# Weight chunks of 1 MB that arrive in one transfer on one semaphore, in a one-core Trainium2 decoder layer

## The reference

```python
m = silu(c) @ w_ada + b_ada                          # 6 parts of 2048: shift, scale, gate, twice
h = rms_norm(x, g_pre) * (1.0 + scale) + shift
q, k, v, u = split(h @ w_in)                         # 4 x 1024 columns
attn = differential_attention(rotary(q), rotary(k), v, cache_k, cache_v, page_table)   # 8 heads
pooled = windowed_means(u, state_pool) @ w_pool
x = x + gate * rms_norm(concat(rms_norm(attn), pooled) @ w_out, g_post)
h = rms_norm(x, g_pre_ffn) * (1.0 + scale2) + shift2
x = x + gate2 * rms_norm(square(relu(h @ w_ff1)) @ w_ff2, g_post_ffn)   # 2048 -> 8192 -> 2048
```

## Time and profile before

| | |
|---|---|
| median of 3 runs | 1516.92 us (1516.67 to 1517.27) |
| the profiled execution, its own time | 1515.74 us |
| its span in the trace | 1514.1 us |
| PE busy | 1454.0 us, 96% of the span |
| DVE / ACT / POOL busy | 54% / 34% / 7% |
| DMA | 316.22 MB, mean 209 GB/s |
| transfers of the stream | 544 of 512 KB, median 4.9 us from issue to landing |

### The profile page before, as it was taken

One profiled execution on the slowest core, in us unless ns is written; L12 is line 12 of the kernel. 1 busy time (PEld: TensorE's weight loads), 2 busy tenths in 40 slices (PEclk: granted clock), 3 DMA queues, 4 the chain that ended last, 5 costly groups with the idle time before them and its releaser, 6 DMA issues.

```text
span 1514.1 us, 27154 instructions
## 1 busy us (share of the span) xinstructions
PE 1454.0 (96%) x10302; PEld 1322.7 (87%) x10302; DVE 810.3 (54%) x1289; ACT 518.3 (34%) x743; POOL 106.2 (7%) x175
## 2 busy tenths in 40 slices
PE   5999999999899998999999999999999999999994
PEld 1677777778688886999998999999999999999993
DVE  2555558855755568665343544333454434555556
ACT  2222234443455543333323333322333322333331
POOL 1000000067310000000000000000000000000003
PEclk9999999999999999999999999999999999999997
DMA  9999989889587667344445544445544444444421
GB/s 367 331 322 328 318 299 323 278 305 358 209 300 265 242 240 273 121 157 149 156 139 199 191 145 160 144 160 190 188 152 150 155 140 148 157 139 150 156 83 69
DMA packets 87725, 316.22 MB, mean 209 GB/s; under 512 B 12160, under 2 KB 12288, under 8 KB 87024
## 3 DMA queue, kind: packets, MB, share of 16 engines
q1 hardware_dynamic: 79056, 287.87, 54.8%
q0 software_dynamic: 5216, 22.51, 3.9%
q10 hardware_dynamic: 3392, 5.01, 0.9%
HBM read 309.56 MB, written 5.80 MB: 208 GB/s over the span
## 4 chain that ended last, share of the span: by engine, by line
PE 85%; DVE 6%; DMA 5%; issue 1%; ACT 1%; SPq 0%; POOL 0%; POOLq 0%; DVEq 0%; ACTq 0%
PE bank L1471 69%; PE bank L1529 7%; PE bank L1449 4%; DMA raw<-in_stream 4%; DMA k_pages<-in_kc 1%; DVE w_lo L760 1%; PE bank L1675 1%; PE bank L1458 1%; PE bank L1704 1%; ACT w_hi L387 0%; DVE back L325 0%; DVE x L326 0%; DVE pair L1153 0%; PE bank L1626 0%; DVE mixed L1141 0%
## 5 line engine op out<-in xcount | busy, mean ns | idle before, releaser
L387 ACT ACTIVATE w_hi<-raw 128x1024 fp32r<-128x1024 f32 x352 | 361.9, 1055 | 360.7 <-PE bank L1471 233.2
L760 DVE TENSOR_TENSOR w_lo<-raw,w_hi 128x1024 fp32r<-128x1024 f32 x352 | 419.5, 1225 | 119.6 <-ACT w_hi L387 118.4
L1471 PE MATMUL bank<-m_hi,w_hi 128*128 128x320 f32 x1280 | 397.3, 310 | 1.2 <-DVE w_lo L760 0.6
L1471 PE MATMUL bank<-m_hi,w_lo 128*128 128x320 f32 x1280 | 395.5, 309 | 0.0
L1471 PE MATMUL bank<-m_lo,w_hi 128*128 128x320 f32 x1280 | 395.5, 309 | 0.0
L1471 PE MATMUL bank<-h_hi,w_hi 128*128 128x320 f32 x1216 | 380.2, 313 | 3.1 <-ACT relu L661 3.1
L1471 PE MATMUL bank<-h_hi,w_lo 128*128 128x320 f32 x1216 | 376.4, 310 | 0.0
L1471 PE MATMUL bank<-h_lo,w_hi 128*128 128x320 f32 x1216 | 376.3, 309 | 0.0
L1471 PEld LDWEIGHTS bank<-m_hi,w_hi 128*128 128x128 f32 x1280 | 240.3, 188 | 15.2 <-issue 13.7
L1471 PEld LDWEIGHTS bank<-h_hi,w_hi 128*128 128x128 f32 x1216 | 228.8, 188 | 27.4 <-issue 27.4
L1471 PEld LDWEIGHTS bank<-m_lo,w_hi 128*128 128x128 f32 x1280 | 240.3, 188 | 0.0
(11 more groups left out here) (230 smaller groups left out, 1024.2 us busy)
## 6 DMA issues: line engine op xcount, KB each, us to landing
raw<-in_stream SPq DMA_DIRECT2D x544, 512.0 KB, 4.9
k_pages<-in_kc POOLq DMA_DIRECT2D x16, 512.0 KB, 10.1
v_pages<-in_vc POOLq DMA_DIRECT2D x16, 512.0 KB, 7.6
x<-in_x_cm ACTq DMA_DIRECT2D x1, 2560.0 KB, 12.1
x<-in_x_cm POOLq DMA_DIRECT2D x1, 2560.0 KB, 11.7
v_out<-v_cm POOLq DMA_DIRECT2D x1, 1280.0 KB, 9.5
k_out<-back POOLq DMA_DIRECT2D x1, 1280.0 KB, 10.1
y_out<-x SPq DMA_DIRECT2D x2, 640.0 KB, 3.0
```

The costliest lines, as they stand in the source:

```text
L387: act.activation(w_hi[2 * (j % 2) + h][:, :], raw[slot][:, h * 1024:(h + 1) * 1024], ACT.Copy).then_inc(hi_ready, 1)
L760: dve.tensor_tensor(w_lo[q][:, :], raw[slot][:, h * 1024:(h + 1) * 1024], w_hi[q][:, :], ALU.subtract).then_inc(slot_used[slot], 1)
L1471: last = pe.matmul(bank[j % 2][:, 0:T], w[q][:, k * P:(k + 1) * P], v[:, 8 * h + k, :], start=(h == 0 and k == 0 and n == 0), stop=(h == 1 ...
```

## The change

SP issues one transfer of 1 MB for each chunk instead of two of 512 KB, and a slot has one semaphore for loading instead of two. Both halves of ACT's rounding and all four products of an ada chunk wait for that one semaphore, that is for the whole chunk. All counts, the slots, the order of instructions on PE, ACT, DVE and POOL, and the wait of SP before it issues stay as they are. On SP a turn of the loop over four slots has 4 transfers where it had 8, each with rows of 8 KB for a partition where it had 4 KB.

```diff
-    raw_loaded = [[S(f"raw_loaded{s}_{h}") for h in range(2)] for s in range(4)]
+    raw_loaded = [S(f"raw_loaded{s}") for s in range(4)]
...
                 sp.wait_ge(slot_used[s], 2 * i + 2)
-                for h in range(2):
-                    half = slice(h * 1024, (h + 1) * 1024)
-                    sp.dma_start(raw[s][:, half], stream[ds(4 * i + s, 1), :, half].rearrange("a p n -> p (a n)")).then_inc(
-                        raw_loaded[s][h], 16)
+                sp.dma_start(raw[s][:, :], stream[ds(4 * i + s, 1), :, :].rearrange("a p n -> p (a n)")).then_inc(
+                    raw_loaded[s], 16)
...
         def hi_half(c4, use, off, j, h):
             slot, u = use_of(use, off)
-            act.wait_ge(raw_loaded[slot][h], 16 * (u + 1))
+            act.wait_ge(raw_loaded[slot], 16 * (u + 1))
...
             for kk in range(4):
-                if kk % 2 == 0:
-                    pe.wait_ge(raw_loaded[slot][kk // 2], 16 * (u + 1))
+                if kk == 0:
+                    pe.wait_ge(raw_loaded[slot], 16 * (u + 1))
```

## The result

The changed kernel takes **1520.53 us** (median of 22 runs, 1516.33 to 1524.85), the kernel before, run beside it on the same chip, 1516.32 (22 runs, 1511.21 to 1520.61). One run of the changed kernel took 2044 us at a granted clock of 0.65 and is left out of the comparison. The profiled execution took 1522.03 us, its span is 1520.4 us; that is 6.3 us more than the profiled execution of before, and somewhat more than the 4.2 us between the medians.

The account below looks back on a forecast made before the run. PE was taken to set the time, from 43 to 212 us only just ahead of the transfers. Terms of 0.3, 4.0, 2.0, 1.1 and 1.0 gave 8.4 us on 1515.74, a median of 1525.3, range 1517.5 to 1531.5.

Parts of the forecast that it names:

- the pages: K pages at 368.25 us: waiting longer beside the stream's 8 KB rows, 1.0 us, bounds 0 and 2.5.
- the first half's lateness: Whole stream: a chunk's first half is usable only when all has landed; slower, 1521 to 1531 us, chance 0.6.
- start: PE's first product at 43.55 us, behind its chunk's first half: 0.3 us later, bounds 0 and 1.2.
- quarters: 43 to 212 us: PE's columns wait where their slack is less than d; 4.0 us, bounds 0.5 and 7.
- q columns: At 208.91 and 231.84 us, where ACT waited for a half: 2.0 us together, bounds 0.5 and 2.5.
- When all of it lands: Stream: a whole chunk lands 5.1 us after issue, 0.15 us before the second half now; bounds 0 and 0.5.
- d: Quarters: the delay of what stands behind DVE's pair, which ends at 113.20 instead of 112.26 us: 0.94 us.
- the row size gives little: DMA queues from 6 to 12 us: 4 KB and 20 KB rows both cost 0.039 us for a KB.
- rival B: Quarters: loss hidden as PE's slips empty the DMA queue; +1 to +3 us, about 1518.5, chance 0.19.
- rival C: Stream: one transfer saves a fixed part, some 0.9 us a chunk; faster, about 1512.5 us, chance 0.09.
- The first chunk of the output projection: Issued at 418.90 us, with PE starting at 434.70 right after ACT and DVE: 1.1 us, bounds 0.7 and 1.3.
- rival D: Pages, second `x` load, ACT's outputs wait longer beside 8 KB rows, quarters reach upper bound: 1531 to 1535 us, chance 0.12.

Follow-up runs that it names:

- the thinned pages: Changed kernel, and kernel before, each with pages bringing 64 of 1024 columns from the third sequence on: 1512.50 us (ratio 0.9988) and 1513.33 us (0.9993).
- the two others with 8 KB rows: The changed kernel with SP's wait ahead of each issue repeated six times, and 24 times: 1521.81 us (ratio 1.0039) and 1529.31 us (1.0094).

## Why the prediction came out as it did

The time forecast was 1525.3 us with a range of 1517.5 to 1531.5; 1520.53 lies in it, and slower was given 0.73. By its own reasons it was mostly wrong, and that the time lies in the range is luck: the terms that made up 6.3 of its 8.4 us were not there (PE is 2.4 us ahead at 306 us), and the smallest but one, 1.0 for the pages, was several times its size (8.3 us from 306 to 435 us).

**The mechanism of the first half's lateness was right, and even its size, for a chunk that lands when the prediction thought.** The kernel with the old transfers and the whole wait has such a chunk: it lands 5.16 us after its first issue, forecast 5.1. PE is 7.3 us behind with it at 306 us, where the sum had 6.3 (start, quarters and q columns), though it was shared out otherwise: 2.4 at the start instead of 0.3, 2.5 in the quarters instead of 4.0, 2.4 after them instead of 2.0. What the sum did not have is another 6.3 us after 435 us.

**The step that failed is "When all of it lands".** It gave the single transfer a gain of 0.15 us, with 0.5 as the bound. Alone it gains 0.4, and the chunk of the earlier trace rows shows this at one place. The changed kernel issues it at 103.1 us. SP's two issues from 103 to 104 us, the first of them this chunk's (4.7), then ACT and DVE:

```profile
DMA to landing us min/median/max: 4.7/5.5/6.3
```

```profile
107.88 2.01 ACT L385 ACTIVATE w_hi<-raw 128x1024 fp32r<-128x1024 f32 x2 [7.73 <-DMA raw<-in_stream]
```

```profile
108.98 2.36 DVE L758 TENSOR_TENSOR w_lo<-raw,w_hi 128x1024 fp32r<-128x1024 f32 x2 [5.22 <-ACT w_hi L385]
```

The chunk is there 4.7 us after its issue, and DVE's pair ends at 111.34, 8.23 us after the issue; before it ended at 112.26, 7.66 after it. So d was 0.57 us here, not 0.94, and the air of 0.9 took it. But most places are not like this one. The lone chunk of the earlier trace rows was the wrong one to measure: in the quarters the median chunk takes 7.15 us before and 5.65 after, 1.5 less, and less than the first half alone took before, 5.87 us (both from the transfers' records). There d is negative, by the distances of the lone chunk some -0.3 us (an estimate: 5.65 + 3.56 to the end of DVE's pair, before 7.15 + 2.36). Where chunks stand in a queue, two transfers of 4 KB rows hold it longer; the share of the DMA engines fell from 0.92 to 0.83. The step "the row size gives little" rested on the earlier trace rows, six microseconds with two queues at work. The rows of q1 from 43.5 to 212 us, where it has the engines nearly alone, are before, with one transfer of 4 KB rows, and after:

```profile
q1 hardware_dynamic: 14800, 53.87, 91.3%
```

```profile
q1 hardware_dynamic: 13892, 53.56, 85.6%
```

```profile
q1 hardware_dynamic: 7374, 53.62, 82.2%
```

For the same bytes that is a tenth less time on the engines, 0.169 us for 4 KB instead of 0.187 (share times 16 engines times 168.5 us, by the bytes). The kernel between has 0.176: the single transfer gives 0.011 of it and the longer rows 0.007, so the row size does give little, some 4%. What the step left out is what two transfers in place of one cost in a queue.

**The quarters, 4.0 us, and the q columns, 2.0,** therefore came out as nothing or a small gain: PE is 1.7 us further ahead at 214 us than at 45, and level from there to 306. That is rival B's outcome for the quarters, though for another reason than B's (a queue that empties as PE slips), and part of rival C's saving: C wanted 0.9 us a chunk to make the kernel faster, and 0.4 alone and 1.5 in the queue came. The Trainium skill's rule quoted with it ("DMA: Bandwidth & Descriptors", "Anatomy of one DMA"), some 2 us fixed for a transfer and 436 GB/s, would by an estimate give 4.4 us for a chunk alone; 4.8 was measured, between it and the forecast's 5.1. The statement "I would be wrong if PE's idle time in the quarters doesn't grow" came true.

**The start, 0.3:** -0.6 at 45 us, not told from 0. **The first chunk of the output projection, 1.1:** from its issue to PE's start there are 16.6 us (424.05 to 440.64), before 15.8, so 0.8; right.

**The pages, 1.0 with 2.5 as the bound, are the step that carried the loss.** The mechanism stood there, turn by turn and packet by packet, and the queues confirm it. The size failed in three ways. It counted one K page load on the path, and V pages and POOL's later ones came too. It counted two chunks beside the pages. But while both queues have work the pages lose a third of their rate, 0.14 MB in a us instead of 0.21, and four transfers of K pages issued together (two sequences', two pages each) are 2.1 MB: by an estimate from these rates 15 us instead of 10 if the stream is there all along. And it had no term for the clock, which was down at 363 us, after PE had waited. From 347 to 363 us the changed kernel loses 5.2 us, of which 2.7 are there at 360 us, where the K pages have just come, and 2.5 are lost in the 3 us of work behind them, at half clock; from 397 to 405 us it is 3.9. This is rival D's first half (pages and other queues waiting longer) with rival B's quarters. D was priced 1531 to 1535 because it was added to the forecast's terms; by itself it is 1521.

That the 8 KB rows beside the pages cause the loss is shown, by the kernel in which only those rows are shorter and by the thinned pages. How the 8 us divide between waiting and clock is read from one execution, and the two others with 8 KB rows lose 7.1 and 3.4 at somewhat different places. That two issues of 4 KB rows make a queued chunk later by 0.9 to 1.1 us than one issue is measured; by what, no run here tells. The 6.3 us that the kernel with two transfers and the whole wait loses after 435 us are unexplained too.

## What to carry to other kernels

A wait that is made coarser must be priced with the landing time of the new transfer in the queue in which it will stand, not with that of a lone one: here 0.7 us on each issue is worth 9 us, and the wait by itself cost 15, while the larger transfer gave 11 of it back with the old rows, and all that was lost up to 306 us with the long ones. Longer rows made a queue a little faster (4% of the engines' time) and its neighbour a third slower, as queues took turns by packets: where small transfers of another queue are on the path, keep the stream's rows no longer than theirs, and try the long rows where the stream is alone; that they gain there isn't shown by a time here. And a range that is hit says nothing of its terms: compare one matmul's start in both traces at every change of stage.

## What the hardware did that was not expected

- Two transfers of 512 KB to 64 partitions each (8 KB rows) ran at 220 GB/s with the DMA engines busy throughout, where two of 512 KB to 128 partitions (4 KB rows) ran at 322: 13% on the whole kernel. The Trainium skill's page "SBUF — State Buffer" ("Door 1: The DMA port swizzle") has partitions 0 to 63 and 64 to 127 on different eights of the 16 ports, so that either half reaches only eight; that would explain it. The trace agrees as far as it goes: an 8 KB row takes 0.61 us of an engine instead of 0.34; no run here tests it further.
- Some 3 us without work for PE were followed by a stretch at the lower clock, but not everywhere: in the changed kernel PE was busy 6.93 us from 350 to 360 us, and the clock of 360 to 370 us was 0.73. In the kernel before it was busy 9.36 us from 350 to 360, and the clock stayed at 1.00. With two transfers of 4 KB rows beside the pages it was busy 6.67 us from 390 to 400, and the clock stayed at 1.00 as well.
- Repeated waits on a semaphore that is already there cost SP about 0.03 us each (5 more: 0.17; 23 more: 0.73).
